# A two-layer trunk step with PEER expert gathers: a block's index selection in pieces of two, two and four heads instead of four and four

## The reference, cut to what matters

```python
def peer_ffn(h, wq, keys, u_tab, v_tab):
    q = (h @ wq).reshape(B, S, PEER_HEADS, 2, half)
    s = jnp.einsum('bshcd,hckd->bshck', q, keys).astype(jnp.float32)
    s_top, i_top = lax.top_k(s, PEER_TOPK)
    cand = (s_top[..., 0, :, None] + s_top[..., 1, None, :]).reshape(B, S, PEER_HEADS, PEER_TOPK * PEER_TOPK)
    best_s, best_i = lax.top_k(cand, PEER_TOPK)
    e1 = jnp.take_along_axis(i_top[..., 0, :], best_i // PEER_TOPK, axis=-1)
    e2 = jnp.take_along_axis(i_top[..., 1, :], best_i % PEER_TOPK, axis=-1)
    experts = e1 * PEER_N_KEYS + e2
    gates = jax.nn.softmax(best_s, axis=-1).astype(h.dtype)
    ...
        u = jnp.take(u_tab, eb, axis=0)
        act = jax.nn.gelu(jnp.einsum('td,tkd->tk', xb, u))
        return jnp.einsum('tk,tkd->td', gb * act, jnp.take(v_tab, eb, axis=0))
```

## Time and profile before

| what | value |
|---|---|
| median of 3 runs | 2577.61 us |
| the runs | 2572.55 to 2579.4 us |
| span of the profiled execution | 2572.5 us |
| its own time (the lowest of the runs) | 2572.55 us |
| first gather issued | at 221.43 us |
| gathers | 1536, of 512 KB each |
| DVE busy, POOL busy, PE busy | 1655.8, 1465.2, 1759.0 us |

### The profile page before, as it was taken

One profiled execution on the slowest core, in us unless ns is written; L12 is line 12 of the kernel. 1 busy time (PEld: TensorE's weight loads), 2 busy tenths in 40 slices (PEclk: granted clock), 3 DMA queues, 4 the chain that ended last, 5 costly groups with the idle time before them and its releaser, 6 DMA issues.

```text
span 2572.5 us, 24469 instructions
## 1 busy us (share of the span) xinstructions
PE 1759.0 (68%) x8425; PEld 866.7 (34%) x8425; DVE 1655.8 (64%) x4021; ACT 314.7 (12%) x840; POOL 1465.2 (57%) x1543
## 2 busy tenths in 40 slices
PE   5873278978487777436878746797848777606577
PEld 3653153643252421222334234364325333101111
DVE  3448985657986770873646699566699575595421
ACT  1320002310221000100201000231012100000000
POOL 0004456556666565555645655765666666777774
PEclk8887588999659899668789968899866899856799
DMA  6747899999999999999999999999999999999997
GB/s 248 254 157 290 325 413 410 410 382 411 410 363 412 412 410 413 369 414 413 409 415 392 411 339 368 411 411 387 411 410 397 411 411 410 409 409 410 409 410 288
DMA packets 248331, 980.65 MB, mean 381 GB/s; under 512 B 28001, under 2 KB 29681, under 8 KB 232849
## 3 DMA queue, kind: packets, MB, share of 16 engines
q0 software_dynamic: 221184, 805.40, 79.2%
q1 hardware_dynamic: 25296, 172.75, 16.9%
q10 hardware_dynamic: 1728, 0.95, 0.1%
HBM read 976.47 MB, written 2.52 MB: 381 GB/s over the span
## 4 chain that ended last, share of the span: by engine, by line
DMA 36%; DVE 21%; PE 20%; POOL 7%; issue 4%; ACT 1%; DVEq 0%; POOLq 0%; ACTq 0%
DMA expert<-in_experts,eidx_t 22%; DMA expert<-in_experts,eidx 13%; DVE expert L1373 12%; PE acc L843 9%; POOL expert L570 7%; PE mmb L788 3%; PE mmb L737 2%; PE mmb L656 1%; PE ob L764 1%; PE trb L744 1%; PE mmb L646 1%; DVE neg_max L1238 1%; DVE small L1077 1%; DMA wt<-in_w_wq 1%; DVE small L1073 0%
## 5 line engine op out<-in xcount | busy, mean ns | idle before, releaser
L570 POOL DMA_INDIRECT expert<-in_experts,eidx x768 | 730.4, 951 | 707.5 <-DVEq L1363 217.5
L1373 DVE CUSTOM_DVE_ANT_0 expert<-expert,hb 128x1024 f32<-128x1024 f32 x768 | 906.1, 1218 | 291.0 <-DMA expert<-in_experts,eidx 276.8
L843 PE MATMUL acc<-expert,strip 128*32 128x512 f32 x3072 | 780.6, 688 | 261.0 <-DMA expert<-in_experts,eidx_t 253.8
L570 POOL DMA_INDIRECT expert<-in_experts,eidx_t x768 | 731.4, 952 | 371.3 <-issue 191.4
L843 PEld LDWEIGHTS acc<-expert,strip 128*32 128x32 f32 x3072 | 142.5, 117 | 816.9 <-DMA expert<-in_experts,eidx_t 635.5
L788 PE MATMUL mmb<-hT,wt 128*128 128x128 f32 x1536 | 190.8, 285 | 22.8 <-DMA wt<-in_w_wq 13.6
L788 PEld LDWEIGHTS mmb<-hT,wt 128*128 128x128 f32 x1536 | 183.6, 200 | 48.7 <-issue 36.6
L646 PE MATMUL mmb<-wt,hT 128*128 128x244 f32 x768 | 178.9, 396 | 11.5 <-DMA wt<-in_w_win 9.4
L646 PEld LDWEIGHTS mmb<-wt,hT 128*128 128x128 f32 x768 | 156.2, 206 | 38.1 <-issue 16.1
L626 PE MATMUL mmb<-mods,sel 128*128 128x512 f32 x224 | 120.1, 665 | 38.2 <-ACT rows L860 36.4
L737 PE MATMUL mmb<-area 32*128 32x384 f32 (+5 forms) x240 | 115.2, 593 | 28.2 <-ACT area L982 23.8
(11 more groups left out here) (178 smaller groups left out, 1566.3 us busy)
## 6 DMA issues: line engine op xcount, KB each, us to landing
wt<-in_w_wq SPq DMA_DIRECT2D x48, 1152.0 KB, 8.4
wt<-in_w_mod SPq DMA_DIRECT2D x48, 1024.0 KB, 8.1
wt<-in_w_win SPq DMA_DIRECT2D x32, 976.0 KB, 8.0
wt<-in_w_wout SPq DMA_DIRECT2D x24, 1024.0 KB, 8.0
expert<-in_experts,eidx POOLq DMA_INDIRECT x768, 13.4
expert<-in_experts,eidx_t POOLq DMA_INDIRECT x768, 13.7
wt<-in_w_uq SPq DMA_DIRECT2D x6, 384.0 KB, 6.4
x<-in_x_sample SPq DMA_DIRECT2D x2, 512.0 KB, 11.8
```

The source lines that it names most:

```text
L570: pool.indirect_dma_start(expert[:, g % RING, :], None, table, bass.IndirectOffsetOnAxis(at, 0)).then_inc(landed[g % RING], 16)
L843: m = pe.matmul(acc[32 * i:32 * i + 32, cs], strip[:, i, at:at + 32], expert[:, (g + i) % RING, cs], start=k < 4, stop=False, skip_group_c ...
L1373: v.tensor_tensor_reduce(expert[:, r, :], expert[:, r, :], hb[:], 1.0, 0.0, ALU.mult, ALU.add, dots[:, k:k + 1]).then_inc(dot_ready, 1)
```

## The change

The constant PICKS = ((0, 2), (2, 2), (4, 4)) gives three pieces of the selection: heads 0 and 1, heads 2 and 3, and heads 4 to 7. `pick` now has six steps in place of four. Steps 0 and 1 come right after `topk` 1, steps 2 and 3 right after `topk` 3, steps 4 and 5 at the end. `idx_ready` counts to three in a pass. POOL waits for it before u slots 0, 32 and 64. The prologue of the first pass is still cut after `pick` 1, which now stands after two heads. The cost table gets numbers for the new steps, so `weave` places gathers a little differently all through the list.

```diff
+PICKS = ((0, 2), (2, 2), (4, 4))
...
-        "ln_h": (5.2, 2.5), "route": 1.5, "topk": 4.7, "pick": (4.4, 6.5, 4.4, 6.5), "fin": (1.3, 6.5, 2.5), "idx_t": 1}
+        "ln_h": (5.2, 2.5), "route": 1.5, "topk": 4.7, "pick": (2.6, 4.4, 2.6, 4.4, 4.4, 6.5), "fin": (1.3, 6.5, 2.5), "idx_t": 1}
...
-        if n - 2 == R_HEADS // 2 - 1:
-            out += [("pick", l, s, b, i) for i in (0, 1)]
-    return out + [("topk", l, s, b, R_HEADS - 1)] + [("pick", l, s, b, i) for i in (2, 3)] + [("idx_t", l, s, b, 0)]
+            for j, (h0, cnt) in enumerate(PICKS):
+                if n - 2 == h0 + cnt - 1:
+                    out += [("pick", l, s, b, 2 * j), ("pick", l, s, b, 2 * j + 1)]
+    last = 2 * len(PICKS)
+    return out + [("topk", l, s, b, R_HEADS - 1)] + [("pick", l, s, b, i) for i in (last - 2, last - 1)] + [("idx_t", l, s, b, 0)]
...
+            if kind == "u":
+                run = min([run] + [h * TOPK - k for h, _ in PICKS if h * TOPK > k])
...
-                    if kind == "u" and k % HALF == 0:
-                        halves += 1
-                        pool.wait_ge(idx_ready, halves)
+                    if kind == "u" and k in [TOPK * h for h, _ in PICKS]:
+                        picks += 1
+                        pool.wait_ge(idx_ready, picks)
...
-                    pe.wait_ge(idx_ready, 2 * (3 * l + b + 1))
+                    pe.wait_ge(idx_ready, len(PICKS) * (3 * l + b + 1))
...
-                    routed = n("routed", 2) - 2
+                    routed = n("routed", len(PICKS)) - len(PICKS)
...
-                    half = gate[:, part(l, b), e // 2 * SLOTS // 2:(e // 2 + 1) * SLOTS // 2]
-                    act.activation(half, half, ACT.Exp).then_inc(gate_exp, 1)
+                    h0, cnt = PICKS[e // 2]
+                    some = gate[:, part(l, b), h0 * TOPK:(h0 + cnt) * TOPK]
+                    act.activation(some, some, ACT.Exp).then_inc(gate_exp, 1)
...
-                    i, nh = e % 2, R_HEADS // 2
-                    h0 = e // 2 * nh
+                    i, (h0, nh) = e % 2, PICKS[e // 2]
+                    equal = eq[:, 0:nh]
```

More of the change, by code:

```diff
@@ L546, in _ @@
             pool.memset(strip[:], 0.0).then_inc(strip_zero, 1)
-            halves = 0
+            picks = 0
             at_idx = {}
@@ L1338, in _ @@
                     link(v.tensor_copy(bf[:, sl], bit[:, sl]))
-                    link(v.tensor_tensor(eq.rearrange("p h k i -> p (h k) i"),
+                    link(v.tensor_tensor(equal.rearrange("p h k i -> p (h k) i"),
                                          iota[:].unsqueeze(1).to_broadcast([P, nh * TOPK, 16]),
                                          bf[:, sl].unsqueeze(2).to_broadcast([P, nh * TOPK, 16]), ALU.is_equal))
-                    link(v.tensor_tensor(eq, eq, i16f[:, h0:h0 + nh, i, :].unsqueeze(2).to_broadcast([P, nh, TOPK, 16]),
+                    link(v.tensor_tensor(equal, equal, i16f[:, h0:h0 + nh, i, :].unsqueeze(2).to_broadcast([P, nh, TOPK, 16]),
                                          ALU.mult))
-                    link(v.tensor_reduce((e1, e2)[i][:, sl], eq.rearrange("p h k i -> p (h k) i"), X, ALU.add))
+                    link(v.tensor_reduce((e1, e2)[i][:, sl], equal.rearrange("p h k i -> p (h k) i"), X, ALU.add))
                     if i == 1:
@@ L1353, in _ @@
                         link(v.tensor_copy(eidx[:, part(l, b), sl], e1[:, sl]))
-                        v.tensor_copy(e1_twice[:, 2 * h0 * TOPK:2 * (h0 + nh) * TOPK].rearrange("p (i c) -> p i c", i=2),
+                        c0 = h0 * TOPK % HALF
+                        v.tensor_copy(e1_twice[:, h0 * TOPK // HALF * P:h0 * TOPK // HALF * P + P]
+                                      .rearrange("p (i c) -> p i c", i=2)[:, :, c0:c0 + nh * TOPK],
                                       e1[:, sl].unsqueeze(1).to_broadcast([P, 2, nh * TOPK]))
```

## The result

The changed kernel has a median of 2587.5 us (8 runs, 2582.8 to 2600.5), the kernel before 2569.8 us in 8 runs beside it. The ratio is 1.008, with a 95% interval of 1.0053 to 1.0107. Measured again on one chip beside the experiments, it was 1.0049 (1.0019 to 1.0079). All ratios here are those on record; the ratio of two medians differs from them by up to 0.0023 (here it would be 1.0069). The prediction had 2575 us, a gain of 2.4 us on 2577.6 us, and gave 0.19 to a loss of this size. The kernel before, in the eight runs beside the change, is itself 7.8 us faster than those 2577.6 us, so the time of 2587.5 us still lies just inside the range of 2564 to 2588, but the change costs some 18 us.

What follows compares the result with a forecast made beforehand. The prediction took DMA transfers to bound the kernel. Start, packing, repair and later passes summed as -2.4 + 3 - 3 + 0 = -2.4 us on the median 2577.6, giving 2575.2 us; 8-in-10 range 2564 to 2588.

Steps and rivals of the forecast that it cites:

- What bounds the kernel: Whole kernel: bound by DMA transfers, so what counts is how early they begin and how much DMA time goes idle.
- The first gather and the piece: Start of first pass: a two-head piece takes 6.8 us, and the first gather comes 17.4 us earlier, at 204.0 us.
- What VectorE does with it: First pass: VectorE stays the limit, the earlier gathers spread over its same time; last piece ready at 307.5 us.
- the rival that keeps 17 us: First pass: transfers bound from the first gather, all 17.4 us come off, 2560 us; chance 0.23 with its milder form.
- The net gain: Start of first pass: restart 15.5 us later, 14 more gathers worth 17.9 us; gain 2.4 us, bounds 0 and 6.
- The rest of the first weave: First pass behind `idx_t`: steps packed more closely cost 3 us, a mended wait near 540 us gains 3 us.
- a packing cost of 3 us: First pass: side work behind `idx_t` starts 16 us later and is packed closer; cost 3 us, bounds 0 and 8.
- a repair of 3 us: First pass, v slots behind `gelu` 1: four come before the transpose, regaining the lost 3 us, bounds 0 and 3.
- The slower rival: First pass: `idx_t` releases PE 16 us later; 2593 us if all is lost, 2586 us if half; chance 0.19.
- The five later passes: Later passes: the added piece's 3.3 us each hide behind a 7.54 us wait, and shifted steps cost 0.
- the shift of steps: Later passes: new costs move steps by up to 5 slots, 8 around `pick`; taken as 0, bounds -6 and +6.
- The added waits: First pass: GpSimd's wait at slot 32 has 3 us to spare; ACT's extra wait for `gate_diff` makes nobody late.

Runs made afterwards that it cites:

- g4: The changed kernel with cost 0 for all `pick` steps, against the kernel before: ratio 0.9945, 2561.0 us on the faster chip.
- f2: The changed kernel with three pieces in the first pass alone, two in later passes, against the kernel before: ratio 0.9987, 2571.7 us on the faster chip.
- f3: The changed kernel with the prologue cut after the second piece, not the first, against the kernel before: ratio 1.0011, 2577.0 us on the faster chip.
- f4: The changed kernel with cost 0 for the first piece, later passes' steps at their old slots, against the kernel before: ratio 1.0013, 2578.9 us.
- g2: The changed kernel's places, but an empty first piece and the old work in the five later passes, against the kernel before: ratio 1.0069, 2587.7 us.
- e2: The changed kernel with the prologue cut after the second piece, not the first, against the kernel before: ratio 0.9896 on the slower chip.

## Why the prediction was wrong, by its steps

**What bounds the kernel: right.** The 21.5 us of the change were found again as idle transfer time, to 0.3 us. Counted in the same way beside before, the other profiles close to 1.5 us, and g4 to 2.3 us.

**The first gather and the piece: right.** The piece took 196.22 - 189.44 = 6.8 us, as predicted from the row of 512 columns. From the first `topk` to the first gather there were 221.43 - 183.57 = 37.9 us before and 196.56 - 176.09 = 20.5 us after, 17.4 us less, as predicted. The landing wait was 7.15, not 6.1 us.

**What VectorE does with it: right, a little too kind.** The last piece was to end 307.5 - 183.6 = 123.9 us after the first `topk`, and ended after 302.8 - 176.1 = 126.7 us (107.9 before). The early start is spread over the same VectorE time, so the rival that keeps 17 us was rightly thought unlikely. The net gain was put at 2.4 us and came out as 11.6 - 11.3 = 0.3 us, 2.1 us less; the last piece was 2.8 us later than forecast. That the loads of `w_wq` now run beside gathers may have a share in it; no run shows one.

**The rest of the first weave: wrong.** I had a packing cost of 3 us and a repair of 3 us. The repair did not come: the v slots behind `gelu` 1 now start at 538.05 us directly behind the transpose (537.64 us), as the list said, yet the rate at 540 us is 209 GB/s. Both had been judged by the order around that transpose alone. The measured loss was 10.7 us, where +3 and -3 us had been put down. f2, with `idx_t` as late as in the change, lost 0.7, and f3, with `idx_t` back at slot 32 and the cost table of the change kept, lost nothing (3.0 beside 5.5 us). The slower rival had the sign and one half of the mechanism: the late release of TensorE costs here only together with the new costs of `pick`, and 10.7 us, not 16. Why the two cost so much together stays open.

**The five later passes: wrong, and this is the step that failed.** I costed the added piece at nothing, behind a wait of 7.54 us at the turn of a pass, and that was right: f4 makes it in every pass at no loss. But I wrote off the shift of steps "by up to 5 slots here and by 8 around `pick`" as 0 with bounds of -6 and +6. It cost 10.8 us in the later passes, and it is one of the two things without which the 10.7 us of the first are not there. I had listed the shifts and had the weak slices in the earlier trace rows, and did not put the two together. A cost table that charges 3.1 us more for `pick` in a pass (24.9 instead of 21.8) takes slots away from every other step of it. Of the 10.8 us, 7.8 lie at two places where this puts one more TensorE step ahead of v slots whose buffers GpSimd is waiting for: `heads` 19 ahead of slot 328 and `route` 2 ahead of slot 960. Both could have been read from the two lists. That these steps are the cause rests on the waits in nine profiles and on f4 and g2; no run moved them alone. For the rest, and for what g4 gains beyond before, I have a reading that is argued and not shown by a run of its own: the chain that ends in `h_t` 2 (slot 388 to 383, 1172 to 1167) has fewer gathers beside it, and TensorE does nothing in a `pick`, so the gathers placed there have nothing of it to run beside. f2 and g4 show the effect of whole sets of places, not of one.

**The added waits: right.** GpSimd never waited for the second or third piece, and g2, which in the later passes has no third exponential, is as slow as the change.

## What to carry to other kernels

When a static interleaving is planned from a cost table, a new step's cost moves every other step; compare the two lists at the weak stretches of the profile before reading the new step's own price, look for steps that have moved ahead of the work that gives buffers back, and test places and work apart (an empty step with the cost, and the step with no cost). The busy time that a step costs is not what the table should charge by itself: charging nothing for `pick` beat both kernels, 0.9945 (0.992 to 0.997) with three pieces on the faster chip. An earlier start is worth only what the engine that was busy in it can spare.

## What was not expected of the hardware

Executions part in the prologue, which is the same in all these kernels up to the first `topk`, by the clock that TensorE is granted. In the ten profiles on the faster chips it was 0.54, 0.71, 0.80 to 0.81 (three) or 1.00 (five) of full speed over 100 to 140 us, while TensorE was busy 39.0, 35.7, 35.6 to 35.8 and 34.5 of 40 us, and the first `topk` came at 194.5, 189.6, 183.5 to 184.7 and 176.1 to 177.0 us. And the chip matters: the unedited kernel before takes 2571 us on one and 2800 us on another (medians of 31 and of 17 to 23 runs), where it moves its 981 MB 9% more slowly, and the late cut (edit of e2) gave 1.0011 (0.998 to 1.0041) on the first and 0.9896 (0.986 to 0.9932) on the second.
